# Projecting the first token tile inside the attention loop, and loading the expert rows one tile at a time

## What is computed

```python
def trunk_layer(x, mod, p, l, latent, ctx_k=None, ctx_v=None):
    ...
    attn = attend_blocked(q, k_all, v_all)
    attn = rms_norm(attn.reshape(B, L, N_HEADS, HEAD_DIM), ...)
    hyo = hyena_mixer(hy, ...)
    hyo = rms_norm(hyo.reshape(B, L, HY_GROUPS, HY_GROUP_DIM), ...)
    mix = jnp.concatenate([attn, hyo], axis=-1) @ p['w_out'][l]
    x = layer_norm(DEEPNORM_ALPHA * x + g1 * mix, ...)
    h2 = x * (1 + sc2) + sh2
    moe = hier_moe(h2, ...)
    x = layer_norm(DEEPNORM_ALPHA * x + g2 * moe, ...)
    return x, k, v
```

## Time and profile before

| what | us |
|---|---|
| median of 3 runs (1629.69 to 1631.33) | 1631.18 |
| the profiled execution: its own time | 1625.72 |
| the profiled execution: its span | 1623.9 |
| TensorE busy in the span | 1490.7 |
| VectorE / GpSimd / ScalarE busy | 933.0 / 384.6 / 360.9 |

### The profile page before, as it was taken

The page is one execution under the profiler, slowest core; times in us unless marked ns, Lnnn a source line. Parts: engine busy times, 40 slices in busy tenths (PEclk is TensorE's granted clock), DMA queues, the critical chain, the costliest instruction groups (busy, mean ns, idle before and its releaser), DMA issues. The chain is left out here.

```text
span 1623.9 us, 22617 instructions
## 1 busy us (share of the span) xinstructions
PE 1490.7 (92%) x8510; PEld 1076.3 (66%) x8510; DVE 933.0 (57%) x1537; ACT 360.9 (22%) x696; POOL 384.6 (24%) x624
## 2 busy tenths in 40 slices
PE   7699998999998899989999988999399999999985
PEld 3466766444444688867888874555388888888852
DVE  4867964466646999987666642534633434333327
ACT  2554232111110111144566540000000000000003
POOL 0441340111110000002325343664222121212204
PEclk9899999999999999999999988999599999999998
DMA  9412214233321312202200002212378998898845
GB/s 304 182 65 82 68 52 136 83 117 113 104 91 44 116 53 66 72 1 79 108 1 1 2 15 91 65 65 91 122 263 327 324 336 328 329 340 312 313 171 215
DMA packets 102742, 229.25 MB, mean 141 GB/s; under 512 B 12807, under 2 KB 70759, under 8 KB 93896
## 3 DMA queue, kind: packets, MB, share of 16 engines
q1 hardware_dynamic: 78680, 195.73, 34.2%
q0 software_dynamic: 10736, 19.77, 3.5%
q10 hardware_dynamic: 13248, 12.72, 2.3%
HBM read 204.66 MB, written 38.98 MB: 150 GB/s over the span
## 5 line engine op out<-in xcount | busy, mean ns | idle before, releaser
L1145 PE MATMUL PS<-buffer 128*128 128x128 f32 (+6 forms) x5638 | 1249.9, 379 | 85.8 <-DVE buffer L1674 22.3
L1145 PEld LDWEIGHTS PS<-buffer 128*128 128x128 f32 (+2 forms) x5638 | 865.5, 194 | 443.4 <-issue 309.0
L1674 DVE TENSOR_TENSOR buffer<-buffer 128x256 f32<-128x256 f32 (+14 forms) x414 | 239.1, 610 | 14.2 <-ACT buffer L990 7.1
L1674 DVE TENSOR_TENSOR buffer<-PS,buffer 128x512 f32<-128x512 f32 (+2 forms) x143 | 94.4, 690 | 143.0 <-PE PS L1145 109.7
L1148 PE MATMUL PS<-buffer 128*128 128x128 f32 (+1 forms) x1176 | 162.4, 281 | 11.7 <-DMA buffer<-moe_inputs,buffer 5.6
L1148 PEld LDWEIGHTS PS<-buffer 128*128 128x128 f32 (+1 forms) x1176 | 135.5, 153 | 39.4 <-issue 29.2
L1674 DVE TENSOR_TENSOR buffer<-buffer,PS 128x256 f32<-128x256 f32 (+3 forms) x55 | 27.6, 502 | 209.7 <-PE PS L1145 199.3
L1037 ACT ACTIVATE buffer<-buffer 128x1152 f32<-128x1152 f32 (+1 forms) x72 | 83.8, 1163 | 115.1 <-DVE buffer L2153 114.9
L2153 DVE TENSOR_SCALAR_CACHE_REDUCE buffer<-PS 128x1152 f32<-128x1152 f32 (+1 forms) x72 | 89.1, 1237 | 24.8 <-PE PS L1145 23.8
L1115 ACT ACTIVATE buffer<-PS 128x256 f32<-128x256 f32 x33 | 12.7, 383 | 366.9 <-PE PS L1145 300.3
L1490 PE MATMUL PS<-buffer 128*64 128x128 f32 x1168 | 80.3, 282 | 7.3 <-ACT buffer L1072 6.1
(11 more groups left out here) (178 smaller groups left out, 965.6 us busy)
## 6 DMA issues: line engine op xcount, KB each, us to landing
buffer<-in_exp_w_gate SPq DMA_DIRECT2D x33, 1024.0 KB
buffer<-in_exp_w_up SPq DMA_DIRECT2D x33, 1024.0 KB
buffer<-in_exp_w_down SPq DMA_DIRECT2D x33, 1024.0 KB
buffer<-in_w_mod SPq DMA_DIRECT2D x24, 1024.0 KB, 6.9
filter_spectra<-buffer ACTq DMA_DIRECT2D x88, 128.0 KB, 1.7
buffer<-filter_spectra SPq DMA_DIRECT2D x44, 256.0 KB, 2.6
buffer<-in_w_in SPq DMA_DIRECT2D x9, 1024.0 KB, 5.4
buffer<-expert_outputs SPq DMA_DIRECT2D x4, 1536.0 KB, 16.8
```

The source lines that it names most:

```text
L1145: return nc.tensor.matmul(out, lhsT, rhs, start=start, stop=stop)
L1674: return dve.tensor_tensor(out, a, b, op)
```

## The change

The first part moves all of the out-projection of tile 0 forward. `turn_mix(0)` stands behind `turn_probs(64)` and writes bank 1 where it wrote bank 0; ScalarE's `copy_mix(0)` stands in step 64 of its own loop. The 16 matmuls are `project_first`: the first half's eight go one into each of the steps 65 to 71, ahead of the step's transposes, and one behind the last values; the second half's first two go ahead of `sum_squares(8)`, the other six between it and `spread_scales(8)`. The second part replaces the four parts of the last load by nine single tiles on four semaphores in turn: from tile 4 on, SyncE waits for the tile four before to have landed.

```diff
--- before.py
+++ after.py
@@ -367,7 +367,7 @@
         xgT = ex.take(2 * KT * P, "p (r k n) -> p r k n", r=2, k=KT)
 
 
-        YG_PARTS = ((0, 1), (1, 3), (3, 6), (6, 9))
+        YG_RING = 4
         fin = Columns(nc, U0, TAIL0)
         yg_first = fin.take(6 * 2 * D, "p (r c n) -> p r c n", r=6, c=2)
         yg_last = Columns(nc, PROBS0, PROBS0 + 3 * 2 * D).take(3 * 2 * D, "p (r c n) -> p r c n", r=3, c=2)
@@ -449,6 +449,7 @@
             return 16 * (at // 2 + 1)
 
         ATT = [(h, t) for t in range(NTILE) for h in range(HEADS)]
+        FIRST_CTX = NLAT * HEADS
 
         PAIRS = NTILE * HEADS // 2
         VALUES_A = {8 * t + 2 * j + 2: 4 * t + j for t in range(NTILE) for j in range(4)}
@@ -628,9 +629,11 @@
             for u in range(2):
                 sp.wait_ge(sem(f"y_scattered{u}"), 16 * pairs + 32)
             y_rows = y_d[0:2 * T, :].rearrange("(c t p) n -> c p t n", c=2, p=P)
-            for part, (t0, t1) in enumerate(YG_PARTS):
+            for t in range(NTILE):
+                if t >= YG_RING:
+                    sp.wait_ge(sem(f"yg_loaded{t % YG_RING}"), 32 * (t // YG_RING))
                 for c in range(2):
-                    load(yg(t0, t1)[:, :, c, :], y_rows[c, :, t0:t1, :], f"yg_loaded{part}")
+                    load(yg(t, t + 1)[:, 0, c, :], y_rows[c, :, t, :], f"yg_loaded{t % YG_RING}")
             for t in range(NTILE):
                 sp.wait_ge(sem("y_ready"), t + 1)
                 out = O["lat"][P * t:P * (t + 1), :] if t < NLAT else O["ctx"]
@@ -1060,6 +1063,12 @@
             def gain_w_out(k):
                 act.activation(w_out[:, k, :], w_out[:, k, :], ACT.Copy, scale=out_gain[:, k:k + 1]).then_inc(sem("w_out_gained"), 1)
 
+            def copy_mix(t):
+                act.wait_ge(sem("mix_transposed"), t + 1)
+                if t >= 2:
+                    act.wait_ge(sem("mix_product"), t - 1)
+                act.copy(mixT[:, t % 2, :, :].rearrange("p k n -> p (k n)"), bank(int(t == 0))).then_inc(sem("mixT_ready"), 1)
+
             exponent(0)
             for i in range(len(ATT)):
                 if i + 1 < len(ATT):
@@ -1076,6 +1085,8 @@
                     square_attention(SQUARE_AT[i])
                 if i - 2 in SQUARE_AT:
                     copy_sums(SQUARE_AT[i - 2])
+                if i == FIRST_CTX:
+                    copy_mix(0)
                 if GAIN_AT <= i < GAIN_AT + KT:
                     act.wait_ge(sem("out_w_loaded"), 32)
                     gain_w_out(i - GAIN_AT)
@@ -1083,13 +1094,6 @@
             square_attention(NLAT)
             copy_sums(NLAT)
 
-            def copy_mix(t):
-                act.wait_ge(sem("mix_transposed"), t + 1)
-                if t >= 2:
-                    act.wait_ge(sem("mix_product"), t - 1)
-                act.copy(mixT[:, t % 2, :, :].rearrange("p k n -> p (k n)"), bank(0)).then_inc(sem("mixT_ready"), 1)
-
-            copy_mix(0)
             for step in range(NTILE + 2):
                 if step + 1 < NTILE:
                     copy_mix(step + 1)
@@ -1508,6 +1512,27 @@
                                                 start=True, stop=True, tile_position=(0, HD * u))
                 last.then_inc(sem("scales_spread"), 1)
 
+            def turn_mix(t):
+                pe.wait_ge(sem("mix_normed"), t + 1)
+                if t:
+                    pe.wait_ge(sem("mixT_ready"), t)
+                for k in range(4):
+                    last = turn(bank(int(t == 0), P, at=P * k), U[0][:, t, P * k:P * (k + 1)])
+                last.then_inc(sem("mix_transposed"), 1)
+
+            def project_first(c, ks):
+                if ks[0] == 0:
+                    pe.wait_ge(sem("attn_scaled"), 1)
+                    pe.wait_ge(sem("w_out_gained"), KT)
+                    pe.wait_ge(sem("out_w_loaded"), 32)
+                if ks[-1] >= 4:
+                    pe.wait_ge(sem("mixT_ready"), 1)
+                for k in ks:
+                    lhsT = attnT[:, 0, k, :] if k < 4 else mixT[:, 0, k - 4, :]
+                    last = mm(bank(4 + c), lhsT, w_out[:, k, 512 * c:512 * (c + 1)], k == 0, k == KT - 1)
+                if c == 1 and ks[-1] == KT - 1:
+                    last.then_inc(sem("mix_product"), 1)
+
             pe.wait_ge(sem("rows_copied"), 4)
             pe.wait_ge(sem("scores_side_copied"), 2)
             scores(0)
@@ -1518,27 +1543,27 @@
                     values(VALUES_A[i], 0)
                 if i in VALUES_B:
                     values(VALUES_B[i], 1)
+                if i > FIRST_CTX:
+                    project_first(0, (i - FIRST_CTX - 1,))
                 turn_probs(i)
+                if i == FIRST_CTX:
+                    turn_mix(0)
                 if i in SUM_AT:
                     sum_squares(SUM_AT[i])
                 if i in SPREAD_AT:
                     spread_scales(SPREAD_AT[i])
             values(PAIRS - 1, 0)
+            project_first(0, (KT - 1,))
+            pe.wait_ge(sem("probsT_d"), len(ATT))
+            project_first(1, (0, 1))
             sum_squares(NLAT)
+            project_first(1, range(2, KT))
             spread_scales(NLAT)
 
-
-            def turn_mix(t):
-                pe.wait_ge(sem("mix_normed"), t + 1)
-                if t:
-                    pe.wait_ge(sem("mixT_ready"), t)
-                for k in range(4):
-                    last = turn(bank(0, P, at=P * k), U[0][:, t, P * k:P * (k + 1)])
-                last.then_inc(sem("mix_transposed"), 1)
 
             def project_mix(t):
                 pe.wait_ge(sem("mixT_ready"), t + 1)
-                pe.wait_ge(sem("attn_scaled"), t + 1 if t == 0 else NTILE)
+                pe.wait_ge(sem("attn_scaled"), NTILE)
                 if t >= 2:
                     pe.wait_ge(sem("resid_ready"), t - 1)
                 for c in range(2):
@@ -1566,15 +1591,12 @@
             pe.wait_ge(sem("max_ready"), len(ATT))
             pe.wait_ge(sem("probsT_a"), len(ATT))
             pe.wait_ge(sem("probsT_d"), len(ATT))
-            turn_mix(0)
-            pe.wait_ge(sem("w_out_gained"), KT)
-            pe.wait_ge(sem("out_w_loaded"), 32)
             for t in range(NTILE + 2):
                 if t + 1 < NTILE:
                     turn_mix(t + 1)
                 if t >= 2:
                     turn_h2(t - 2)
-                if t < NTILE:
+                if 1 <= t < NTILE:
                     project_mix(t)
                 if t >= 2:
                     route(t - 2)
@@ -1641,9 +1663,7 @@
                 for h in range(2):
                     mm(mixed(t)[:, 512 * h:512 * (h + 1)], upper, x1[:, t, 512 * h:512 * (h + 1)], True, False)
             for t in range(NTILE):
-                for part, (t0, t1) in enumerate(YG_PARTS):
-                    if t == t0:
-                        pe.wait_ge(sem(f"yg_loaded{part}"), 32)
+                pe.wait_ge(sem(f"yg_loaded{t % YG_RING}"), 32 * (t // YG_RING + 1))
                 if t >= AN:
                     pe.wait_ge(sem("y_gained"), t - AN + 1)
                 for h in range(2):
```

## The result

The changed kernel took 1610.53 us (median of 4 runs, 1608.98 to 1611.95) against 1630.43 of the kernel before on the same chip (4 runs, 1626.70 to 1631.33): ratio 0.9889, 95% interval 0.9873 to 0.9905 (the two medians alone give 0.9878).

What follows compares the result with a forecast made beforehand. TensorE, busy nine tenths almost throughout, was taken as the bound. Savings of 14.6 us at the attention's end and 1.1 in the last stage made 15.7, giving 1615.5 us from the median 1631.18; range 1612.8 to 1622.5.

Steps and rivals of the forecast that it cites:

- What bounds the kernel, and the first part: Attention's end: TensorE bounds; 16.3 us leave the path behind the last scales, 1.7 us delay ahead, net 14.6 saved.
- The walk through the steps: Context-head steps 64 to 71 and behind: each engine's instructions timed in order; tile 8's scales spread 1.7 us later.
- What is late next: Tile 0's norm behind the attention: inputs for `turn_h2(0)` ready at 998.6, wanted at 999.2; holds by half a us.
- GpSimd's instruction: Tile 0's expert inputs: if it takes 3.31 us for 2.34, TensorE waits some 0.5 once; nothing counted.
- The last stage: Expert-row loads tile by tile: later tiles land ahead of need, and 1.1 us saved reaches the end.
- Both waits: Last stage: TensorE's waits of about 0.54 us ahead of tile 1 and 0.54 ahead of tile 3 go.
- The sum and the number: Whole kernel: 14.6 + 1.1 = 15.7 us saved; 1610.0 on the profiled execution's scale, 1615.5 on the median's.
- the unknowns named there: Steps' small gaps taking up matmuls (1.5 us either way) and last stage paying (0 to 1.1): 1613 to 1618.5.
- both clock rivals: Attention's end: clock falls as before (1622.5 us, chance 0.15) or stays low up to the second tile (1636, 0.02).
- The first: Context-head steps: the clock falls as before at 962.8, about 7 us of the gain lost, 1622.5 us; chance 0.15.
- The norm of tile 0: Behind the attention: inputs 2 us late and last stage gives nothing, 1618.5 us; norm or second part fails, chance 0.09.
- Loads one at a time: Last stage: each pair takes 4.2 us without overlap, stage 3.4 longer, not 1.1 shorter, 1620.0 us; chance 0.04.

Runs made afterwards that it cites:

- that ring: Changed kernel with one tile of loads in flight instead of four: last stage 63.80 us, median 1621.91 us, ratio 0.9961 to the kernel before.

## Why the prediction was right or wrong

**What bounds the kernel, and the first part.** Right. The walk through the steps put single instructions within 0.5 us. Less the 2.93 by which the trace lies later, the transpose of step 65 is at 960.2 (forecast 960.15), the sums of tile 7 at 962.3 (962.35), its spreading at 969.7 (969.9), the last values at 972.4 (972.65), the spreading of tile 8 at 981.6 (981.9), the second tile's projection at 984.5 (985.0). Saved: 14.9 us at this place in the first pair of traces and 15.1 over all, forecast 14.6. Ahead of the scales the matmuls cost 1.4 where I had 1.7: the gaps took a little more of them than I gave them. Two small slips of addition changed nothing that matters: what I listed as left behind the scales adds up to 1.79 and not to the 1.95 written (2.0 was measured), and 3.6 us behind 983.0 is 986.6 and not 986.8.

**What is late next.** Right, and as close as forecast: tile 0's norm started at 986.4 on the old scale (986.8), and the expert inputs were ready some 0.5 us ahead of TensorE (0.6). GpSimd's instruction took 2.35, not 3.31.

**The last stage.** Right. Both waits went, 33.88 less 32.86 is 1.0 of TensorE's time, and about 1.1 reached the end (1.2 in the first pair of traces). SyncE's new wait left no hole, with four tiles or with two.

**The sum and the number.** 15.7 was forecast; the traces show 16.2. The measured median is 5.0 us below the forecast 1615.5, and the step that failed is "on that scale **1615.5 us**": I took 15.7 from 1631.18, the median of three runs, and gave the range only the uncertainty of the mechanism, 2.7 us downwards (the unknowns named there give 1.5). The level itself was uncertain by as much. Later medians of the kernel before are 1628.93 (17 runs), 1628.01 (25), 1627.75 (17) and 1627.62 (12), with single runs from 1624.0 to 1633.99; its profiled execution, at 1625.72, was among the short ones while the changed kernel's, at 1611.95, was the longest of its four. From 1628.0 the same sum gives 1612.3, and 1628.0 - 16.2 = 1611.8, beside measured medians of 1610.5 to 1611.1. So of the 5.0 us some 3.2 are the level, 0.5 the size of the gain, and 1.3 stay open. That the first level was high by chance is the likeliest reading, but no run shows it: three of the four runs behind 1630.43 are the three that gave 1631.18, and against them the gain looks like 18.1 us by the ratio and 19.9 by the medians. I had seen a gap of 5.5 us between the profiled execution and the median and only carried it over; it was a sign that one kernel's runs differ by several us.

**The rivals.** The clock did not fall, so both clock rivals are out for this kernel. The first was a real danger: with the long wait filled and the steps left as they were, it fell, and needed 4.7 us of unbroken matmuls to come back, not the 2.6 on which my working of both rivals leaned. What a fall would have cost the changed order itself is not shown. The norm of tile 0 was not late. Loads one at a time are slow only without overlap: that ring costs 9.4 us, more than the 4.5 by which I had priced the rival from its landing time alone (3.4 longer, not 1.1 shorter), since a pair takes 4.7 to 5.1 and every tile from tile 2 on waits.

## What to carry to other kernels

Work that is ready early is best put into the waits of a dependent chain, one instruction to a step: here seven matmuls in the steps and nine around the last chain cost 1.4 us of delay and took 16.3 off the path. Walk the steps with durations from the trace, and look one stage further for what is late next. And ask how far the level itself scatters before giving a range: a difference that can be placed to 0.1 us between two points of a trace can lie under several us of scatter between runs.

## What was not expected of the hardware

Executions whose first 950 us are the same program differed by up to 5.6 us at 116 us into the program (in one pair of traces, the same four issues of weight loads were done at 20.5 and at 24.2 us), and by 1.6 to 1.7 us each for stretches of 3.4 us at half the clock that came in some executions only, at 120 and 749 us. Such a stretch can also change its place or length: with it the attention's end varied by 0.5 us where nothing was changed in it, and TensorE's part of the last stage by 0.7. In the steps of the context heads TensorE's records cover 84% of the time ahead of the fall (4.55 of 5.4 us), and 97% of the same steps in the changed kernel, where the clock stayed up (5.22 of 5.4 us).
